# Second block in two phases: mixers beside the input projection, then gates, branches and output projection by token halves with the last norm

## The reference, cut to what matters

```python
h = rms_norm(x, g_pre)
proj = h @ w_in + b_in        # 54 tiles of 128 columns, and 8 columns of rates
y_a = gated_delta_rule(...) * silu(a_z)      # 8 chunks of 128 tokens
y_b = silu(layer_norm(conv31(glu))) * silu(b_z)
y_c = window_attention(...) * silu(c_z)
y_d = rg_lru(...) * silu(d_z)
y_e = memory_attention(...) * silu(e_z)
gate = sigmoid(proj_gates)                   # 5 branches x 1024 columns
merged = sum(gate[b] * (y_b @ w_br[b]) for b in 5 branches)
out = x + rms_norm(merged @ w_out, g_post)
```

## Time and profile before

| | us |
|---|---|
| three runs | 3450.47, 3455.75, 3455.55 (median 3455.55) |
| the profiled execution's own time | 3458.23 |
| its span in the trace | 3456.4 |
| PE busy | 3206.3 (93%) |
| DVE, ACT, POOL busy | 1443.4, 1097.4, 669.2 |

### The profile page before, as it was taken

How to read it: one execution, slowest core, us unless ns; L and a number is a source line. 1 busy time by engine, 2 the same in 40 slices (tenths; PEclk the granted TensorE clock), 3 DMA queues, 4 the chain that set the end, 5 groups by cost and what they waited for, 6 DMA issues and landing times. The chain is left out here.

```text
span 3456.4 us, 36380 instructions
## 1 busy us (share of the span) xinstructions
PE 3206.3 (93%) x14817; PEld 2466.1 (71%) x14817; DVE 1443.4 (42%) x1849; ACT 1097.4 (32%) x1632; POOL 669.2 (19%) x317
## 2 busy tenths in 40 slices
PE   6999988879999999995999999999999999999995
PEld 4765544447788888874767787777777888888874
DVE  3113333536414141475456877668552213223123
ACT  4334433323312030342453322223434323223122
POOL 2222111014222222242121000011111222222220
PEclk9999999889999999997999999999999999999997
DMA  3211000013111111123332121104334221221121
GB/s 125 97 63 60 19 0 1 1 64 108 49 49 46 48 48 49 49 89 137 100 108 92 37 68 44 61 34 141 110 110 164 92 98 49 98 98 49 49 92 55
DMA packets 105933, 246.19 MB, mean 71 GB/s; under 512 B 8232, under 2 KB 49448, under 8 KB 105640
## 3 DMA queue, kind: packets, MB, share of 16 engines
q1 hardware_dynamic: 97992, 215.56, 19.3%
q10 hardware_dynamic: 7776, 28.32, 2.0%
HBM read 187.74 MB, written 55.05 MB: 70 GB/s over the span
## 5 line engine op out<-in xcount | busy, mean ns | idle before, releaser
L1676 PE MATMUL psum<-normed_hi,w_hi 128*128 128x512 f32 x1632 | 674.3, 413 | 42.4 <-POOL w_lo L2218 35.2
L1678 PE MATMUL psum<-normed_hi,w_lo 128*128 128x512 f32 x1632 | 639.4, 392 | 0.0
L1677 PE MATMUL psum<-normed_lo,w_hi 128*128 128x512 f32 x1632 | 638.2, 391 | 0.0
L2218 POOL TENSOR_TENSOR w_lo<-buffer,w_hi 128x1024 fp32r<-128x1024 f32 x122 | 310.0, 2541 | 1500.8 <-ACT w_hi L1250 1500.8
L1676 PEld LDWEIGHTS psum<-normed_hi,w_hi 128*128 128x128 f32 x1632 | 308.8, 189 | 114.9 <-POOL w_lo L2218 36.7
L1678 PEld LDWEIGHTS psum<-normed_hi,w_lo 128*128 128x128 f32 x1632 | 307.6, 188 | 66.1
L1677 PEld LDWEIGHTS psum<-normed_lo,w_hi 128*128 128x128 f32 x1632 | 308.9, 189 | 63.7 <-issue 8.0
L2839 POOL TENSOR_TENSOR w_lo<-buffer,w_hi 128x1024 fp32r<-128x1024 f32 x88 | 212.4, 2415 | 724.9 <-ACT w_hi L2757 724.9
L1250 ACT ACTIVATE buffer<-psum,par 128x512 f32<-128x512 f32 (+1 forms) x196 | 138.0, 705 | 518.6 <-PE psum L1678 503.4
L2719 PE MATMUL psum<-hidden_hi,w_hi 128*128 128x512 f32 x512 | 200.9, 392 | 3.1 <-POOL w_lo L2839 3.1
L2719 PE MATMUL psum<-normed_hi,w_hi 128*128 128x512 f32 x512 | 200.1, 391 | 3.3 <-POOL normed_lo L2846 2.2
(11 more groups left out here) (393 smaller groups left out, 5438.5 us busy)
## 6 DMA issues: line engine op xcount, KB each, us to landing
buffer<-in_w_mlp SPq DMA_DIRECT2D x72, 512.0 KB, 3.6
buffer<-in_w_in SPq DMA_DIRECT2D x70, 512.0 KB, 4.9
scratch_in<-buffer ACTq DMA_DIRECT2D x54, 512.0 KB, 2.9
buffer<-in_w_gate SPq DMA_DIRECT2D x40, 512.0 KB, 3.6
buffer<-scratch_in SPq DMA_DIRECT2D x32, 512.0 KB, 6.5
buffer<-scratch_y SPq DMA_DIRECT2D x20, 512.0 KB, 7.7
buffer<-in_w_br SPq DMA_DIRECT2D x20, 512.0 KB, 3.6
buffer<-in_w_o SPq DMA_DIRECT2D x16, 512.0 KB, 3.7
```

The costliest lines, as they stand in the source:

```text
L1676: pe.matmul(out, hi, xh, start=k == 0, stop=False)
L1677: pe.matmul(out, hi, xl, start=False, stop=False)
L1678: mm = pe.matmul(out, lo, xh, start=False, stop=k == unit.kc - 1)
L2218: pool.tensor_tensor(ws.lo[:, n % 2], raw[:, n % 2], ws.hi[:, n % 2].bitcast(F32), ALU.subtract).then_inc(w_lo, 1)
```

## The change

The second block becomes two phases. `mixer_phase` keeps the mixers and the 110 input units, waits at its end for its stores (`ends`), and brings the first two gate weights into the slots. The pace of the units is changed: unit 86, not 74, is due at `T_AFTER`. `merge_phase` is new: gates and branches in the same order of tiles, with six PSUM banks in place of four, the output projection as two passes (8 tiles for the first token half, then 8 for the second, each with a weight slot of its own), and the closing norm woven in by halves. `norm_phase` is gone. The edits of the first block (`row_of`) put the numbers 0 to 7 through a list and change no order.

```diff
-    pace = Pace((0, 0.0), (34, 250.0), (74, T_AFTER), (110, T_MERGE), (st.n_merge, T_MERGE + 654.0),
-                (st.n_merge + 16, T_MERGE + 742.0))
+    pace = Pace((0, 0.0), (34, 250.0), (86, T_AFTER), (len(st.units), T_END))
...
+        self.slots += [("gate", BRANCHES[0] * DC), ("gate", BRANCHES[0] * DC + 1)]
...
+            def ends():
+                yield T_END + 60.0
+                for r in range(3):
+                    sp.wait_ge(stored[r], 16 * ((len(held) + 2 - r) // 3))
...
+class Merge:
+    def __init__(self, tick):
+        self.slots, self.units, self.starts, self.at, self.tick = [], [], [], 0.0, tick
+        for b in BRANCHES:
+            self.starts.append(self.at)
+            for pair in range(DC // 2):
+                tiles = [b * DC + 2 * pair, b * DC + 2 * pair + 1]
+                for tile in tiles:
+                    self.slots.append(("gate", tile))
+                    for h in range(2):
+                        self.add("gate", tile, h, h == 0, DC, 0)
+                self.slots.append(("br", tiles[0]))
+                last = b == BRANCHES[-1] and pair == DC // 2 - 1
+                for n, (t, h) in enumerate([(0, 0), (1, 0), (0, 1), (1, 1)] if last else [(0, 0), (0, 1), (1, 0), (1, 1)]):
+                    self.add("br", tiles[t], h, n == 0, BT, t * BT)
+        self.starts.append(self.at)
+        for h in range(2):
+            for j in range(DC):
+                self.slots.append(("out", j))
+                self.add("out", j, h, True, DC, 0)
...
+def merge_phase(nc, m, d):
+    st = Merge(5.5)
+    N, RING = len(st.units), 6
...
+        def by_pool(j):
+            return j % 2 == 1 and j < DC - 1
...
+                        if unit.kind == "out" and unit.tile == 0:
+                            if k < DC - 2:
+                                pe.wait_ge(merged_lo, k + 1)
+                            else:
+                                pe.wait_ge(half_lo, 2 * unit.half + k - DC + 3)
...
+            def norm():
+                for h in range(2):
+                    yield out_end[h] + 3.0
+                    pe.wait_ge(gathered, (DC - 1) * (h + 1))
+                    if h:
+                        pe.wait_ge(logged, 1)
+                    pe.matmul(n_sum, m.c(C_ONE), total[:, h], start=True, stop=True).then_inc(summed, 1)
...
+            def outputs():
+                for h in range(2):
+                    for j in range(DC):
+                        yield out_end[h] + 5.4 + (2.0 if h == 0 else 0.7) * j
+                        q = h * DC + j
+                        part = halves(out[:, j])[h]
+                        if j == 0:
+                            dve.wait_ge(rooted, h + 1)
+                        dve.scalar_tensor_tensor(part, part, m.p("post_g", j), total[:, h], ALU.mult, ALU.mult).then_inc(scaled, 1)
+                        if not by_pool(j):
+                            dve.wait_ge(scaled, q + 1)
+                            dve.wait_ge(res_in[q % 4], 16 * (q // 4 + 1))
+                            dve.tensor_tensor(part, part, halves(res[:, j])[h], ALU.add).then_inc(done_dve, 1)
...
 def second_block(nc, m, d):
     mixer_phase(nc, m, d)
-    m.clear(top=A_WORK, end=A_ACT)
-    norm_phase(nc, m, m.act, m.act, m.p("post_g", 0, 8), DC, (m.take(2, S), m.take(S)), residual=m.res, out=d["out"])
+    merge_phase(nc, m, d)
```

More of the change, by code:

```diff
@@ L102 @@
 A_WORK = A_SPLIT + 2 * DC * S
+A_Y = A_WORK + 6 * S
+A_T = A_Y + 2 * DC * S
 A_END = 52800
[L104 removed]
 class Split:
@@ L441, in front_phase, with row_of @@
     T = MLA_H * NB
+    rows_order = list(range(NB))
+    def row_of(t):
+        return rows_order[t // MLA_H]
     small = m.take(3, T)
@@ L469, in wide @@
     def wide(t):
-        return max(0, t + 1 - MLA_H * (HALF // P))
+        return sum(row_of(v) >= HALF // P for v in range(t + 1))
     def pair_ready(i):
@@ L1250, in __call__ @@
         return self.act.activation(out, x, func, **more)
-Unit = namedtuple("Unit", "kind tile half slot begins kc at")
+Unit = namedtuple("Unit", "kind tile half slot begins")
 class Stream:
@@ L1650, in gemm @@
                     s = None if unit.slot is None else unit.slot % 2
-                    out = gp[st.bank(n)] if unit.kind != "ab" else gp[st.bank(n)][0:8]
-                    for k in range(unit.kc):
-                        yield pace(n + k / unit.kc)
+                    out = gp[n % 2] if unit.kind != "ab" else gp[n % 2][0:8]
+                    for k in range(DC):
+                        yield pace(n + k / DC)
                         if k == 0:
@@ L2516, in conformer, with add, count, index @@
                     dve.scalar_tensor_tensor(cy[:, j], cy[:, j], m.p("b_ln_g", j), croot, ALU.mult, ALU.mult).then_inc(conf_scaled, 1)
+            woven(prepare(), inverse(), scan(), windows(), band(), lru(), memory(), decay_rates(), conformer(), short_convs(),
+                  long_convs())
+MergeUnit = namedtuple("MergeUnit", "kind tile half slot begins kc at due")
+class Merge:
[18 more added lines that the diff above has]
+                self.add("out", j, h, True, DC, 0)
+        self.done_at = {u.slot: n + 1 for n, u in enumerate(self.units)}
+    def add(self, kind, tile, half, begins, kc, at):
+        self.units.append(MergeUnit(kind, tile, half, len(self.slots) - 1, begins, kc, at, self.at))
+        self.at += self.tick * kc / DC
+    def count(self, kind, n):
+        return sum(u.kind == kind for u in self.units[:n])
+    def index(self, kind, tile, half):
+        return next(n for n, u in enumerate(self.units) if (u.kind, u.tile, u.half) == (kind, tile, half))
+    def end(self, n):
+        return self.units[n].due + self.tick * self.units[n].kc / DC
@@ new lines, in roots @@
+            def roots():
+                for h in range(2):
+                    yield out_end[h] + 3.6
+                    act.wait_ge(summed, h + 1)
+                    run(total[:, h], n_sum, ACT.Ln, bias=m.c(C_EPS, 1), scale=1.0 / D).then_inc(logged, 1)
+                    act.wait_ge(logged, h + 1)
+                    run(total[:, h], total[:, h], ACT.Exp, scale=-0.5).then_inc(rooted, 1)
+            woven(outputs(), roots(), merged_split(), branches(), gates(), weights())
+        @block.gpsimd
```

559 lines of the change are left out of this document (289 added, 270 removed).

## The result

| | us |
|---|---|
| before, five executions | 3450.39 to 3458.23, median 3455.55 |
| changed, five executions | 3461.94 to 3473.19, median 3470.59 |
| ratio | 1.0044, 95% interval 1.0026 to 1.0061 |
| profiled execution of the changed kernel | 3461.94, span 3460.1 |

The change makes the kernel slower by 0.4%, 15 us over the forecast of 3456, on the side that was given 28%. The profiled execution is the fastest of the five, and its span is only 3.7 us over that of before, whose profiled execution (3458.23) was the slowest of its five. So the stages have to be compared one by one. Busy time by stage of the changed kernel (us, engine busy with instructions, granted clock, DMA share, GB/s): delta stage, windows, last input units, gates to output, end.

A forecast was written before the change was run, and what follows sets the result against it. PE was taken as the bound up to 3411.2 us, with a 45.2 us closing norm behind it. Terms 49 - 11 - 15 + 6.5 - 6.6 - 24.8 + 2 = 0 gave 3456 us, range 3434 to 3474.

The forecast's parts named there:

- The pace: Mixer stages, 273 matmuls moved ahead of the windows: delta stage +49, windows -11, last input units -15, together +23 us.
- +2 for the clock: Windows: PE, standing 1.5 to 2 us before each transposes, may lose its clock now and then, +2 us.
- filled holes: Delta stage: moved matmuls fill 13 of PE's 29.8 us idle, mostly waits at L1787, while those at L1798 stay.
- the two hits: Windows: twice a weight split ahead of the exponentials on ACT delays the transposes, 2.8 us each.
- My sign for the delta stage: Check on the profile: first chunk to first transposes near 546 us.
- Rival A: Delta stage fills all its holes: 17 us more gained, 5 in the windows, 3434 us; chance 0.33.
- Rival B: Windows: PE's clock falls as its idle share rises, 26 us more, 3480 us; chance 0.1.
- Rival D: End: POOL or stores lag, the norm's half stays bare, 3465 us; chance within the forecast's spread.
- Rival C: Delta stage: six more weight splits in ACT's queue hold up chain steps, +22, 3478 us; chance 0.12.
- The seam: Between the phases: POOL's split of the second gate weight, then the barrier, leave PE without work, +6.5 us.
- The end: Behind the last output unit: only the second half's norm remains, 20.4 us for 45.2, -25 us.
- Part 3: Gates to output projection: the output projection's starting wait goes, second-pass weight splits hide, gain 6.6 us.

The follow-up runs named there:

- at 74: Changed kernel with unit 74 due at T_AFTER, first-half stores later, last second-half splits behind the weight split, all residual adds on DVE: 3434.49 us, ratio 0.9941.
- at 78: Changed kernel with unit 78 due at T_AFTER, first-half stores later, last second-half splits behind the weight split, all residual adds on DVE: 3452.80 us, ratio 0.9999.
- the half splits: Edit putting the last two tiles' second-half splits 3.1 us later in ACT's list, behind a weight split; alone on the changed kernel: 3463.04 us, ratio 1.0027.
- at 70: Changed kernel with unit 70 due at T_AFTER, first-half stores later, last second-half splits behind the weight split, all residual adds on DVE: 3439.48 us, ratio 0.9954.
- pace 98: Changed kernel with unit 98, not 86, due at T_AFTER, twice the change's step: 3529.41 us, ratio 1.0217.

## Why the prediction missed its likeliest case, step by step

**The pace** was right, term by term: 49, -11 (with +2 for the clock: -9) and -15 were forecast; 3.7 + 46.3 = 50.0, -9.5 and -15.2 came. The order's sign was read rightly too: the waits at L1787 went, those at L1798 stayed. Two sizes inside came out partly by luck. The 13 us of filled holes measured 12, but PE's idle time shows 7 of them only. And of the two hits forecast for the windows one came, while the clock cost more: three stretches of 3.4 us at half clock for one before. My sign for the delta stage, 546 us, also counted the 15 matmuls that stand ahead of it, as A's 525 did not; without them the forecast was 542, and 543.0 came. The chain was the windows' bound, so what left the windows was paid in full in the delta stage. Rival A (all holes filled) did not happen, PE's idle time there fell by 7 of 29.8. Rival B did not at this step of the pace, and did at twice the step. Rival D did not happen. Rival C is a real mechanism, though not at 86 in the delta stage: it costs in two windows at 74, in one at 86 (10.9 us), and its sign stands in four at 78.

**The seam** came as forecast, 6.4 for 6.5.

**The end** too, 19.5 for 20.4, with two errors inside that cancel, which is luck: I took 1.12 for each scale beside POOL, as in the first block, and 0.68 for each add. The eight scales took 0.70 to 0.75, 3.3 us less in all, and three of the adds took 1.63, 2.9 us more.

**Part 3 is the step that failed.** It said -6.6 for gates to output, and +5.4 came. That is 12.0 us, the whole difference between the forecast 0 and the measured 11.6 of the second block. The wait of 4.2 us at the output projection's start did go. But I had costed the cover of the output weights as a rate, 3.5 us of splitting against 5.44 a unit, and looked at no instruction in front of it. PE's waits in the changed kernel from the first gate to the last output unit:

```profile
PE psum L2475 <- POOL w_lo L2574: 6.9, 3, 3.4
...
PE psum L2486 <- DVE buffer L2647: 0.8, 1, 0.8
```

Before, an output weight covered two units. Now it covers one, and 5.44 us don't hide what its split waits for: DVE's backlog at the second unit (3.19), a store that waits for DVE in SP's queue at the fifteenth (3.44), and the sum of the first half (0.84). Each of the two long gaps is followed by PE at half clock, and so is the seam:

```profile
2684.80:2700.00 15.20, 15.19 (x55) 12.29 (x56) 5.83 (x5) 6.37 (x7) 0.00 (x0) 0.80 0.89 346
3345.00:3360.00 15.00, 11.81 (x46) 9.37 (x45) 5.91 (x7) 6.45 (x9) 6.44 (x3) 0.89 0.34 106
3425.00:3435.00 10.00, 7.23 (x25) 5.82 (x26) 4.07 (x2) 3.48 (x6) 5.12 (x2) 0.83 0.33 127
```

At half clock for 40% of 15.2 us, 22% of 15 us and 34% of 10 us, PE lost 3.0, 1.7 and 1.7 us. Against 739.8 us of pure matmuls the stage lost 16.0, where I had left 3.9: 7.7 in the gaps, 3.4 at half clock behind them, 3.0 behind the seam (3.4 forecast), and 1.2 for the product with ones of the first half, which now stands in the stream; 0.7 stays open. The later stores took back 5 to 6 us, and with the half splits and all adds on DVE it was 9 (757.2 to 748.2): 5.6 in the second pass, 2.1 around the second output unit, and 1.3 at the first branch, where the wait varies from 0.25 to 2.10 between profiles.

The remaining 3 us between the second block's +11.6 and the medians' +15 can be the first block, whose part in single executions goes from 1594 to 1604 us over the profiles. That is not shown, as the executions behind the medians were not profiled.

## What to carry to other kernels

Hiding a phase under a matmul stream moves its waits into the queues that feed the stream. List for each queue (a weight's load, its split, its low part) which waiting instruction now stands in front, since a mean rate that fits says nothing of that. Where a dependent chain bounds a stage, moving matmuls out of it gains little (here 9.5 us for 46 us of matmuls) and moving more out costs its clock; look instead at which long instruction of a helper engine stands ahead of the chain's step. And compare stages, not totals, where a part that the change doesn't touch varies by more than the change.

## What the runs showed that I had not expected

- The time of the windows is not monotonic in the pace: 248.6, 238.2, 248.3, 227.2 and 246.3 us at 70, 74, 78, 86 and 98. PE's work bounds it at 70 (idle 5.8 us), ACT's order costs at 74 and, by its sign, at 78, and at 98 the clock is lost.
- In the changed kernel's windows PE was idle for 17%, mostly in pieces of 1 to 2 us, and the mean granted clock was 0.98; at pace 98 it was idle for 29%, in pieces of about 3 us, and the clock was 0.81. A single gap doesn't decide it: behind the same gap of 3.19 us the changed kernel ran at half clock in one profile and at full clock in the other.
- The first block, the same in all kernels, took 1594 to 1604 us; in the changed kernel's profile it had a clock of 0.87 in one stretch of 48 us, in that of before 0.72.
